# The MLPs' down projections by one level of Strassen's algorithm, with the weight sums on GpSimd

## The reference

```python
y = jnp.square(jax.nn.relu(h2 @ w_mlp_in[l])) @ w_mlp_out[l]
x = x + gate2[:, None, :] * y          # first block

def _sqrelu_mlp(h, w1, w2):
    return jnp.square(jax.nn.relu(h @ w1)) @ w2
x = x + _sqrelu_mlp(h, mlp_w1[layer], mlp_w2[layer])   # second block, twice
```

## Time and profile before

| | us |
|---|---|
| median of 3 runs | 1958.76 |
| their range | 1957.43 to 1959.01 |
| the profiled execution's own time | 1959.16 |
| its span in the trace | 1957.3 |

### The profile page before, as it was taken

The page is one execution under the profiler, slowest core; times in us unless marked ns, Lnnn a source line. Parts: engine busy times, 40 slices in busy tenths (PEclk is TensorE's granted clock), DMA queues, the critical chain, the costliest instruction groups (busy, mean ns, idle before and its releaser), DMA issues.

```text
span 1957.3 us, 21184 instructions
## 1 busy us (share of the span) xinstructions
PE 1903.8 (97%) x8624; PEld 1529.1 (78%) x8624; DVE 966.7 (49%) x1391; ACT 751.3 (38%) x1080; POOL 76.7 (4%) x94
## 2 busy tenths in 40 slices
PE   3999999989999999999999999999999999999999
PEld 2777668868888888877788888888877778888887
DVE  7367643554444346554554344445644554344443
ACT  4344443343323244356734232234445534233231
POOL 5100000010000000001100000000001000000000
PEclk9999999989999999999999999999999999999999
DMA  7445533313232223200122232322221122222222
GB/s 255 157 145 183 170 121 113 124 63 101 95 99 95 100 95 113 98 33 33 44 97 94 89 103 91 104 90 97 97 87 43 65 86 97 97 97 97 97 97 76
DMA packets 55121, 197.66 MB, mean 101 GB/s; under 512 B 6400, under 2 KB 6656, under 8 KB 55024
## 3 DMA queue, kind: packets, MB, share of 16 engines
q1 hardware_dynamic: 52272, 188.24, 28.2%
q0 software_dynamic: 2320, 7.31, 1.3%
q10 hardware_dynamic: 432, 0.74, 0.1%
HBM read 194.13 MB, written 2.14 MB: 100 GB/s over the span
## 4 chain that ended last, share of the span: by engine, by line
PE 93%; DVE 4%; ACT 2%; issue 0%; DMA 0%; POOL 0%; DVEq 0%; ACTq 0%
PE ps L252 26%; PE ps L254 25%; PE ps L253 25%; PE ps L288 2%; PE ps L290 2%; PE ps L289 2%; DVE RAW L1222 1%; PE ps L373 1%; PE ps L425 1%; PE ps L584 1%; PE ps L672 1%; DVE WL L1214 1%; PE ps L571 1%; PE ps L602 1%; PE ps L359 1%; PE ps L412 1%
## 5 line engine op out<-in xcount | busy, mean ns | idle before, releaser
L252 PE MATMUL ps<-R0h,WH 128*128 128x512 f32 x1200 | 471.6, 393 | 21.4 <-POOL R0l L1791 18.9
L1214 DVE TENSOR_TENSOR WL<-RAW,WH 128x1024 fp32r<-128x1024 f32 x303 | 372.3, 1233 | 241.0 <-ACT WH L769 237.5
L769 ACT ACTIVATE WH<-RAW 128x1024 fp32r<-128x1024 f32 x303 | 317.2, 1051 | 394.0 <-PE ps L254 339.5
L254 PE MATMUL ps<-R0h,WL 128*128 128x512 f32 x1200 | 468.2, 390 | 0.0
L253 PE MATMUL ps<-R0l,WH 128*128 128x512 f32 x1200 | 468.1, 390 | 0.0
L252 PE MATMUL ps<-R1h,WH 128*128 128x512 f32 x1064 | 420.8, 396 | 7.8 <-POOL R1l L1819 2.8
L253 PE MATMUL ps<-R1l,WH 128*128 128x512 f32 x1064 | 416.8, 392 | 0.0
L254 PE MATMUL ps<-R1h,WL 128*128 128x512 f32 x1064 | 416.7, 392 | 0.0
L252 PEld LDWEIGHTS ps<-R0h,WH 128*128 128x128 f32 x1200 | 225.9, 188 | 76.8 <-issue 16.5
L254 PEld LDWEIGHTS ps<-R0h,WL 128*128 128x128 f32 x1200 | 225.8, 188 | 47.4
L253 PEld LDWEIGHTS ps<-R0l,WH 128*128 128x128 f32 x1200 | 225.9, 188 | 46.1
(11 more groups left out here) (266 smaller groups left out, 1471.0 us busy)
## 6 DMA issues: line engine op xcount, KB each, us to landing
RAW<-in_W SPq DMA_DIRECT2D x351, 512.0 KB, 3.2
XT<-in_X SPq DMA_DIRECT2D x4, 512.0 KB, 7.7
ARENA<-bias_scratch POOLq DMA_DIRECT2D x8, 256.0 KB, 3.3
XT<-in_X POOLq DMA_DIRECT2D x8, 256.0 KB, 3.6
out_x<-XT SPq DMA_DIRECT2D x8, 256.0 KB, 2.0
ARENA<-bias_scratch POOLq DMA_DIRECT2D x8, 128.0 KB, 3.2
con<-in_CON POOLq DMA_DIRECT2D x1, 578.0 KB, 5.6
CSB<-in_CV ACTq DMA_DIRECT2D x1, 512.0 KB, 6.1
```

Of the source, the lines that this page charges most:

```text
L252: e.matmul(ps(b), wh, hi, start=first, stop=False)
L254: return e.matmul(ps(b), wl, hi, start=False, stop=last)
L769: e.activation(WH[:, n % NHL, :], RAW[:, i % NRAW, :], ACT.Copy).then_inc(sem["w_hi"])
L1214: e.tensor_tensor(WL[:, s, :], RAW[:, i % NRAW, :], r32(WH[:, s, :]), ALU.subtract).then_inc(sem["w_lo"])
```

## The change

In all three MLPs the way out of a block (hidden 1024 x model 1024) is cut into four pairs of output tiles, p = 0 to 3. The product of a pair is one 2x2 block product: the weight [512+512 hidden] x [128+128 model], the hidden activations [512+512 hidden] x [256+256 tokens]. It is done with seven products instead of eight (Winograd's form of Strassen's algorithm), each 4 x 3 = 12 matmuls of 256 columns: 28 products in a block, in the order `DOWN`, 3 x 4 x 28 x 12 = 4032 matmuls of 256 columns in all.

- **Weights.** A pair of chunks gives four units to split instead of two: `a` (A11 and A12), `s1` (A21+A22 and A22), `s3`, and the half-sized `s4`. Their sums are four GpSimd subtractions or additions of 128x512 a pair (`weight_sums`), 3 x 16 x 4 = 192 in all. Units of even pairs are stored in the buffers A, which the hidden activations have left, those of odd pairs in `WH` and `WL` slots.
- **Activations.** The hidden tiles n and n + 4 follow each other on the way in (`UP`). For each such pair VectorE forms three further combinations of 256 columns and one more (four, in three instructions), so that 1792 columns instead of 1024 are copied as high parts by ScalarE and subtracted by VectorE, into the new `HC`, which lies in ARENA.
- **Results.** Each of the 28 products is read from PSUM by VectorE and added to a 128x256 half of an `XT` tile; the next product of the same bank is then added on top of it in PSUM where the sum is wanted (M3, M4, M6, M7 don't clear the bank), and waits for that read.
- The order of `hi` and `lo` is written out anew: 10 units in the way in (`UP_UNITS`) and 14 in the way out (`DOWN_UNITS`) of each block.

The core of the diff (the rest renames counters):

```diff
+UP = (0, 4, 1, 5, 2, 6, 3, 7)
...
-            out += [(tag + "i", 8 * b + n) for n in range(8)] + [(tag + "o", 8 * b + n) for n in range(8)]
+            out += [(tag + "i", 8 * b + n) for n in UP] + [(tag + "o", 8 * b + n) for n in range(8)]
...
+OUTS = ("m0o", "m1o", "m2o")
+UNITS = ("a", "s1", "s3", "s4")
+PROD = {"M1": ("a", 0, 0, 1, 0, 0), "M2": ("a", 1, 2, 2, 0, 0), "M3": ("s4", 0, 3, 2, 0, 1),
+        "M4": ("s1", 1, 6, 3, 1, 0), "M5": ("s1", 0, 1, 1, 1, 1), "M6": ("s3", 1, 4, 2, 0, 1),
+        "M7": ("s3", 0, 5, 3, 1, 1)}
+DOWN = [("M1", 0), ("M5", 0), ("M1", 1), ("M2", 0), ("M3", 0), ("M6", 0),
+        ("M5", 1), ("M6", 1), ("M7", 0), ("M2", 1), ("M4", 0), ("M3", 1),
+        ("M1", 2), ("M7", 1), ("M5", 2), ("M6", 2), ("M4", 1), ("M2", 2), ("M3", 2),
+        ("M1", 3), ("M7", 2), ("M5", 3), ("M6", 3), ("M4", 2), ("M2", 3), ("M7", 3), ("M3", 3), ("M4", 3)]
+POS = {key: n for n, key in enumerate(DOWN)}
+TILE_END = (5, 10, 11, 16, 18, 23, 26, 27)
+UP_UNITS = (0, 2, 1, 1, 1, 2, 2, 1)
+UP_UNITS_FIRST = (0, 0, 0, 1, 1, 2, 2, 2)
+DOWN_UNITS = (1, 2, 5, 6, 10, 11, 13, 14, 16, 18, 20, 24, 25, 27)
+def bank(m, p):
+    return {"M5": WIDE[2], "M3": WIDE[2], "M2": WIDE[3]}.get(m, WIDE[p % 2])
...
+def unit_before(tag, p, u):
+    last = {"a": "M2", "s1": "M4", "s3": "M7", "s4": "M3"}[u]
+    if p % 4 > 1:
+        return (tag, p - 2, last)
+    if p % 4 == 1 and u != "s4":
+        return (tag[:2] + "i", 8 * (p // 4) + UP[{"a": 6, "s1": 5, "s3": 7}[u]])
+    if p >= 4:
+        return (tag, p - 2, last)
+    if tag == "m0o":
+        return None
+    return ({"m1o": "m0o", "m2o": "m1o"}[tag], 14 + p, last)
...
+        HC = [nc.alloc_sbuf_tensor_at("HC" + p, [P, 4, 1792], F32R, offset=arena_at + 4 * 7168 * n)
+              for n, p in enumerate("hl")]
+        SB = ARENA[:, 14336:16384].rearrange("p (a b) -> p a b", a=2)
+        flat = TMP[:].rearrange("p a b -> p (a b)")
+        F1, F2 = [flat[:, 0:768], CSB[:, 0:768]], flat[:, 768:2048]
...
+            def product(tag, p, m, check):
+                u, half, q, phase, _, _ = PROD[m]
+                b = bank(m, p)
+                start = m in ("M1", "M5", "M2")
+                e.wait_ge(sem["w_lo"], LO[tag, p, u])
+                open_bank(b)
+                for k in range(4):
+                    if check:
+                        e.wait_ge(sem["mlp_lo"], 3 * (pair_no(tag, p) // 4 * 4 + k) + phase)
+                    wh, wl = (unit(tag, p, u, v)[:, 512 * half + 128 * k:512 * half + 128 * k + 128] for v in range(2))
+                    xh, xl = (HC[v][:, k, 256 * q:256 * q + 256] for v in range(2))
+                    more = dict(skip_group_check=not start)
+                    e.matmul(ps(b, 0, 256), wh, xh, start=(start and k == 0), stop=False, **more)
+                    e.matmul(ps(b, 0, 256), wh, xl, start=False, stop=False, **more)
+                    t = e.matmul(ps(b, 0, 256), wl, xh, start=False, stop=(k == 3), **more)
+                t.then_inc(sem["mm"])
+                free[b] = (("mlp_x", x_count(tag, p, m)),)
...
+                    for n, (m, p) in enumerate(DOWN):
+                        product(tag + "o", 4 * blk + p, m, n < 12)
...
+                    if key[0] in OUTS:
+                        tag, p, u = key
+                        if u == "a":
+                            i = AT[tag, 2 * p]
+                            e.wait_ge(sem[f"raw{i % NRAW}"], 16 * (i // NRAW + 1))
+                        else:
+                            e.wait_ge(sem["sadd"], 4 * pair_no(tag, p) + {"s1": 2, "s3": 3, "s4": 4}[u])
+                        had = unit_before(tag, p, u)
+                        if had is not None:
+                            e.wait_ge(sem["mm"], MM[had])
+                        e.activation(unit(tag, p, u, 0), unit_raw(tag, p, u), ACT.Copy).then_inc(sem["w_hi"])
...
+                            hi(UP_UNITS[n])
+                            if n % 2 == 0 and g > 1:
+                                e.wait_ge(sem["mlp_lo"], 3 * (g - 2) + 2)
+                            elif n % 2 and g > 0:
+                                e.wait_ge(sem["mlp_lo"], 3 * (g - 1) + 3)
+                            e.wait_ge(sem["mm"], MM[tag + "i", 8 * blk + UP[n]])
...
+                            hi(UP_UNITS[n] if blk else UP_UNITS_FIRST[n])
+                            h = hidden(g, n % 2)
+                            e.activation(h, h, ACT.Square).then_inc(sem["mlp_sq"])
+                        if n % 2 == 0:
+                            e.wait_ge(sem["mlp_t"], 3 * g + 1)
+                            e.activation(HC[0][:, k, 0:512], F1[g % 2][:, 0:512], ACT.Copy).then_inc(sem["mlp_hi"])
                         else:
+                            e.wait_ge(sem["mlp_t"], 3 * g + 2)
+                            e.activation(HC[0][:, k, 512:1280], F2[:, 0:768], ACT.Copy).then_inc(sem["mlp_hi"])
+                            e.wait_ge(sem["mlp_t"], 3 * g + 3)
+                            e.activation(HC[0][:, k, 1280:1792], F2[:, 768:1280], ACT.Copy).then_inc(sem["mlp_hi"])
+                    for n in range(28):
+                        if n in DOWN_UNITS:
                             hi()
-                if then is not None and norm is not None:
+                        if blk == 3 and then is not None and n in TILE_END:
+                            then(TILE_END.index(n))
...
+                def hidden_rest(g, k, phase, src, c0, c1):
+                    e.wait_ge(sem["mlp_hi"], 3 * g + phase)
+                    e.tensor_tensor(HC[1][:, k, c0:c1], src, r32(HC[0][:, k, c0:c1]),
+                                    ALU.subtract).then_inc(sem["mlp_lo"])
+                def way_in(blk, n):
+                    i, k = 8 * blk + n, n // 2
+                    g = pair_no(out, 4 * blk + k)
+                    h, f1 = hidden(g, n % 2), F1[g % 2]
+                    h12, h21, h22 = f1[:, 512:768], F2[:, 0:256], F2[:, 256:512]
+                    if norm is None:
+                        lo(UP_UNITS[n])
+                        e.wait_ge(sem["mlp_rr"], base + i + 1)
+                        e.tensor_tensor(h, h, h, ALU.mult).then_inc(sem["mlp_sq"])
+                    else:
+                        if i == 0:
+                            sums(norm)
+                            lo(2)
+                            e.wait_ge(sem["rb"], BRING[norm])
+                        lo(UP_UNITS[n] if blk else UP_UNITS_FIRST[n])
+                        if n % 2 == 0 and g > 1:
+                            e.wait_ge(sem["mlp_lo"], 3 * (g - 2) + 2)
+                        elif n % 2 and g > 0:
+                            e.wait_ge(sem["mlp_lo"], 3 * (g - 1) + 3)
+                        e.wait_ge(sem["mm"], MM[tag + "i", 8 * blk + UP[n]])
+                        e.scalar_tensor_tensor(h, blocks(ps(WIDE[n % 4]), 2), 0.0, blocks(SQ[:], 2), ALU.max,
+                                               ALU.mult).then_inc(sem["mlp_rr"])
+                    e.wait_ge(sem["mlp_sq"], base + i + 1)
+                    if n % 2 == 0:
+                        e.tensor_tensor(f1[:, 256:512], h12, f1[:, 0:256], ALU.subtract).then_inc(sem["mlp_t"])
+                        hidden_rest(g, k, 1, f1[:, 0:512], 0, 512)
+                    else:
+                        e.tensor_tensor(blocks(F2[:, 512:1024], 2), bcast(h22, 2), blocks(f1[:, 256:768], 2),
+                                        ALU.subtract).then_inc(sem["mlp_t"])
+                        e.wait_ge(sem["mlp_t"], 3 * g + 2)
+                        e.tensor_tensor(F2[:, 1024:1280], h21, F2[:, 512:768], ALU.subtract).then_inc(sem["mlp_t"])
+                        hidden_rest(g, k, 2, F2[:, 0:768], 512, 1280)
+                        hidden_rest(g, k, 3, F2[:, 768:1280], 1280, 1792)
+                def read(p, m):
+                    _, _, _, _, chunk, half = PROD[m]
+                    n = 2 * (p % 4) + chunk
+                    x, src = XT[:, n, 256 * half:256 * half + 256], ps(bank(m, p), 0, 256)
+                    had = read_before(p, m)
+                    if had is not None:
+                        e.wait_ge(sem["mlp_x"], x_count(out, *had))
+                    e.wait_ge(sem["mm"], MM[out, p, m])
+                    if norm is None:
+                        e.scalar_tensor_tensor(x, src, mod_col(40 + n), x, ALU.mult, ALU.add).then_inc(sem["mlp_x"])
+                    else:
+                        e.tensor_tensor(x, src, x, ALU.add).then_inc(sem["mlp_x"])
                 for blk in range(4):
                     for n in range(8):
+                        way_in(blk, n)
+                    for n, (m, p) in enumerate(DOWN):
+                        read(4 * blk + p, m)
+                        if n in DOWN_UNITS:
                             lo()
                         if blk == 3 and then is not None:
+                            if n - 1 in TILE_END:
+                                then(TILE_END.index(n - 1))
+                            if n == 27:
+                                then(7)
```

(18 more changed lines are left out.)

252 lines of the change are left out of this document (136 added, 116 removed).

## The result

The changed kernel takes **2057.9 us** (median of 4 runs, 2054.7 to 2058.8), against 1958.4 us for the kernel before on the same chip: a ratio of 1.0506, 95% interval 1.0487 to 1.0524. It is slower, as forecast, but by 5.1% and not by 1.6%, and it lies above the range.

What follows compares the result with a forecast made beforehand. TensorE, busy 97% of the span, was taken as the bound. 1959.2 - 57.7 (narrow matmuls) + 64 + 17 + 7 (stalls) + some 1.5 gave 1991 us, slower by 1.6%; range 1920 to 2045, likeliest case 1970 to 2025.

Steps and rivals of the forecast that it cites:

- narrow matmuls: TensorE, way out: 4032 matmuls of 256 columns replace 2304 of 512, a gain of 57.7 us.
- TensorE's added waits: Stalls at the way out: 64 us in m1 and m2, 17 in m0, 7 for the last blocks.
- The step that failed: Last term of the sum: some 1.5 us for M3 due earlier and a possible clock dip.
- the worst rival: Every sum costs its 0.9 us and waits lower TensorE's clock: 2050 us, plus up to 20; chance 0.17.
- The pitch: Time per 256-column matmul on TensorE in the way out: taken as 115 ns, between bounds of 105 and 130.
- the split into order and collisions: VectorE's lateness after the way in, m1 and m2: 7.5 us from the handover chain, 4.8 from GpSimd's sums.
- The rival without collisions: GpSimd's sums fit into VectorE's waits and cost nothing: 1932 us, faster; chance 0.2.
- the scalar relu: Way in of m0: relu on ScalarE saves VectorE 0.66 us a tile, ending 4.6 us late instead of 7.5.
- The collisions: Way in: about 11 GpSimd sums meet VectorE's chain, costing 4.8 us a block, about 4.0 in m0.
- The upper bound of 0.9: Most that one GpSimd sum can cost VectorE's chain in the way in: 0.9 us, from engines taking turns.
- Its sign: What would decide for the slowest rival: a mean cost of 0.7 us per GpSimd sum.
- The unit rest: VectorE's mean time for a weight unit's rest would rise from 1.23 us to 1.4 or more.

Runs made afterwards that it cites:

- the kernel with both edits: The changed kernel with GpSimd's weight sums cut to 8 columns and VectorE's unit rests put between the hidden tile's steps in the way in: 1935.6 us.
- The stops-alone kernels: The kernel before, with VectorE held up once per block of m1 and m2 by 16 or 10 dummy multiplications: 2028.1 and 1993.3 us.
- the run almost without sums: The changed kernel with GpSimd's 192 weight sums cut to 8 of their 512 columns, order and semaphores kept: 1961.2 us.

## Why the prediction was wrong in size

Against its own sum, in the same order:

| term | predicted | measured |
|---|---|---|
| profiled execution before | 1959.2 | 1959.2 |
| narrow matmuls | -57.7 | -44.0 (118.4 ns) |
| TensorE's added waits | 64 + 17 + 7 = 88 | 96.4 |
| clock, and waits too short to list | 1.5 | 45.7 (some 35 of it clock) |
| sum | 1991 | 2057.3 |

The profiled execution of the changed kernel took 2057.5.

**The step that failed** is the last one, "some 1.5 because faster products bring M3's due time forward and the clock may dip". The 45.7 is what busy time exceeds 1903.8 - 44.0 = 1859.8 by. In the trace of the changed kernel the stretches at half clock lie over TensorE's busy time for 95.6 us, in that of before for 25.5; half of the 70.1 between is 35 us of clock. The 11 left are waits too short to be listed, of which the kernel with both edits shows some 8. The stops-alone kernels show the cause without Strassen: 2.4 and 1.9 us of surcharge for each stop. The changed kernel has in each of its twelve blocks one stop of 3.9 to 6.6 us, and in eleven of them a second of 1.8 or 1.9. I had written the clock into the worst rival alone, as "plus up to 20", and priced it there too low as well. The earlier trace rows had shown it, 0.83 after waits of a few us: a forecast that puts twelve stalls of 4 to 8 us into dense work must charge each with its half-clock time, some 2 us or more, in the sum and not in the tail. Twelve times 2.4 would still have given only 29 of the 35; the further stops of each block would have to bring the rest, which no run here takes apart.

**The pitch** was mis-sized by 3.4 ns, 13.7 us. The row nearest to the truth was the one of 119 ns, which I had named and set aside by averaging; but it is of 128 columns with a weight load of 64, so its nearness may be chance. The Trainium skill (TensorE: Matmul & The Clock Gate, Back-to-back issue gap) gives 262 cycles, 109 ns; no run here shows that, neither with 118.4 nor with 120.0.

**The stalls** were right in sum (88 against 96.4) and in cause, a VectorE that is through the way in too late: even the split into order and collisions held. They were not right in place (below). The rival without collisions had 31 us of stalls; the run almost without sums shows 25.6. The groups of L660 in the three windows above have 29.0 us of waits in m1 and 31.2 in m2, where I had 34 (with the last block) and 32. In m0 there are 31.6 for my 22: I took the scalar relu to give slack back, and it gave less. That is 7.3 to 7.9 us a block in all three, where I had 8 and, in m0, 4. The collisions were mis-sized in the mean: 0.44 us a sum in my chain (4.8 for 11), while VectorE's busy time has 0.59 over all sums and 0.75 for those of the first pairs. The upper bound of 0.9 rested in part on a misreading: 1.97 us is the pitch of GpSimd's four instructions (7.88 / 4), the three unit rests give 5.86 / 3 = 1.95, and no row gives the 1.07; 1.95 - 1.23 is 0.7. A smaller slip without effect: ScalarE's idle time before conversions is 394.0 us, not 396.

**The worst rival** named 2050 and up to 20 more, and the measured 2057.9 lies there, but by luck. Its stalls were 149 us where 96.4 came, its narrow matmuls gained 57.7 where 44.0 came, and its clock cost up to 20 where some 35 came; the errors cancel. Its sign, a mean of 0.7 us per sum, is met by the first pairs' sums (0.75) and not by all (0.59).

**Where** the waits were: "in the first seven products, released by VectorE's reads or by rests of hidden tiles, not by weight units" held (64.1 HCl, 22.9 bank, 5.4 and 3.0 XT, 1.4 WL). But in the block shown the longest stop stood in the very first product and not before M3, whose bank wait was to be nearly the whole stall: sums of pair 1 fall between rests (1100.09, 3.28 for two) and make VectorE late before the way out begins. GpSimd's means (1453 to 1901 ns, 1606 over all, for some 1.7 us) and its sum (308 for 300) held, and so did the pitch (118.4 within 111 to 120). The unit rest did not: of its full-sized forms in the way out (L1395) the mean is 1.34 us, for 1.4 or more.

**Covers.** Transfers stayed hidden: chunks land in 3.6 us for 3.2, and no wait of TensorE names one. The collisions are of one kind: VectorE's reads (L1653, one operand in PSUM) took 404 to 426 ns in all 224 cases, and the relu (L1628) 676 to 692; the rests, with both operands in SBUF, went from 677 up to 2058:

```profile
L1653 DVE TENSOR_TENSOR XT<-ps,XT x224: 404/417/426, 1117.3 to 2052.6; 128x256 f32<-128x256 f32 x112
L1628 DVE SCALAR_TENSOR_TENSOR TMP<-ps,SQ x48: 676/684/692, 1071.4 to 2008.3; 128x512 f32<-128x512 f32 x48
L1605 DVE TENSOR_TENSOR HCl<-TMP,HCh x120: 677/958/2058, 431.6 to 2013.7; 128x512 fp32r<-128x512 f32 x72, 128x768 fp32r<-128x768 f32 x48
```

(minimum, median and maximum in ns.) The Trainium skill says this too (SBUF — State Buffer, Who interferes with whom): a VectorE instruction with at most one SBUF input, outside the modes that use two ports, doesn't contend with GpSimd, one with two does when GpSimd's reads SBUF. The trace agrees (417 ns at the median with one, up to 2058 with two).

## What to carry to other kernels

A wait put into dense TensorE work costs its length and a surcharge: here 1.9 us after 2.6 and 2.4 after 6.3, paid in busy time, where a table of waits doesn't show it. So compare busy time and mean clock first, and count stops, not only their microseconds.

Work given to an idle engine isn't free if it gets in the way of the one that sets the pace: here 0.6 us of VectorE for each 1.3 us sum. Such a saving has to be weighed together with the order: here the order of instructions alone won back the whole loss of 99.5 us, and nothing beyond it.
